# The attention loop of a hybrid encoder block, written out for its four head pairs

## The reference, cut to what matters

```python
MLA_HEADS, QK_NOPE_DIM, QK_ROPE_DIM, V_HEAD_DIM, CHUNK, Q_BLOCK = 8, 64, 32, 64, 64, 128
q = (rms_norm(q_c, q_norm_g) @ w_uq).reshape(B, S, H, 64 + 32)
kv = rms_norm(kv_c, kv_norm_g)
k_nope, v = kv @ w_uk, kv @ w_uv                  # per head 64 and 64 columns
...                                               # rotary part of q and k
s = (qn @ k_nope.T + qr @ k_rope.T) * sm_scale    # float32
s = where(key_chunk <= query_chunk, s, -1e30)     # block-causal, chunks of 64
out = softmax(s) @ v                              # per head and block of 128 queries
```

## Time and profile before

| | us |
|---|---|
| median of 3 runs | 2049.97 (2049.68 to 2051.54) |
| profiled execution | 2049.59 |
| its span, first to last instruction | 2047.8 |
| of which attention's steps | about 484 to 1105 |
| PE busy over the span | 1854.8 (91%) |
| DVE, ACT, POOL busy | 1220.7, 728.3, 499.6 |

### The profile page before, as it was taken

One profiled execution on the slowest core, in us unless ns is written; L12 is line 12 of the kernel. 1 busy time (PEld: TensorE's weight loads), 2 busy tenths in 40 slices (PEclk: granted clock), 3 DMA queues, 4 the chain that ended last, 5 costly groups with the idle time before them and its releaser, 6 DMA issues. The chain is left out here.

```text
span 2047.8 us, 27274 instructions
## 1 busy us (share of the span) xinstructions
PE 1854.8 (91%) x8738; PEld 1438.2 (70%) x8738; DVE 1220.7 (60%) x2093; ACT 728.3 (36%) x1209; POOL 499.6 (24%) x550
## 2 busy tenths in 40 slices
PE   2899999997999999999996999983999999999970
PEld 2677878764666666666664788872899999999960
DVE  4688889856675675675674655546344444444434
ACT  3545353325444444444443332320222222222214
POOL 0131413112211211211221111103234343434330
PEclk8999999997999999999998899985999999999995
DMA  7655656410000000000002434414799999999948
GB/s 275 203 176 153 202 139 181 144 56 1 9 8 6 8 8 5 8 8 5 8 8 100 174 139 145 159 73 154 240 271 275 271 270 278 267 280 270 276 98 328
DMA packets 216160, 290.79 MB, mean 142 GB/s; under 512 B 24373, under 2 KB 172048, under 8 KB 215834
## 3 DMA queue, kind: packets, MB, share of 16 engines
q1 hardware_dynamic: 193498, 220.60, 32.5%
q0 software_dynamic: 20224, 69.22, 13.5%
q10 hardware_dynamic: 2368, 0.17, 0.1%
HBM read 229.13 MB, written 60.82 MB: 142 GB/s over the span
## 5 line engine op out<-in xcount | busy, mean ns | idle before, releaser
L905 PE MATMUL tbank<-probs,VV 128*128 128x512 f32 (+3 forms) x640 | 292.5, 538 | 1.3 <-ACT probs L1123 1.2
L987 DVE TENSOR_REDUCE cmax<-tbank 128x1 f32<-128x512 f32 (+2 forms) x340 | 206.0, 606 | 99.1 <-PE tbank L830 91.9
L1123 ACT ACTIVATE probs<-tbank 128x512 f32<-128x512 f32 (+1 forms) x320 | 169.7, 533 | 235.3 <-PE tbank L876 231.6
L387 PE MATMUL pbank<-hhi,wslhi 128*128 128x512 f32 x512 | 205.9, 402 | 8.2 <-DVE wsllo L440 6.8
L874 PE MATMUL tbank<-Qhi,Khi 97*128 97x512 f32 (+2 forms) x321 | 212.4, 662 | 0.0
L1881 DVE TENSOR_SCALAR xTe<-ebank,modcol 128x256 f32<-128x256 f32 (+1 forms) x128 | 53.8, 473 | 258.8 <-PE ebank L1799 137.5
L1149 POOL TENSOR_SCALAR diag<-cst,nmax 128x128 fp32r<-128x128 f32 x138 | 84.4, 612 | 486.1 <-DVE nmax L990 485.8
L387 PE MATMUL pbank<-hhi,wsllo 128*128 128x512 f32 x512 | 200.7, 392 | 0.0
L387 PE MATMUL pbank<-hlo,wslhi 128*128 128x512 f32 x512 | 200.6, 392 | 0.0
L1821 PE MATMUL ebank<-xTe,wg 128*128 128x192 f32 x1024 | 171.8, 326 | 3.1 <-DVE ahi L1909 1.8
L1821 PEld LDWEIGHTS ebank<-xTe,wg 128*128 128x128 f32 x1024 | 167.9, 190 | 7.9 <-DVE ahi L1909 2.1
(11 more groups left out here) (273 smaller groups left out, 3491.4 us busy)
## 6 DMA issues: line engine op xcount, KB each, us to landing
wg<-in_w_exp_gate SPq DMA_DIRECT2D x32, 1024.0 KB, 6.3
wu<-in_w_exp_up SPq DMA_DIRECT2D x32, 1024.0 KB, 9.6
wd<-in_w_exp_down SPq DMA_DIRECT2D x32, 1024.0 KB, 7.4
wraw<-in_w_in SPq DMA_DIRECT2D x60, 512.0 KB, 4.1
wmod<-in_w_ada POOLq DMA_DIRECT2D x64, 256.0 KB, 3.4
xt<-in_x SPq DMA_DIRECT2D x4, 2048.0 KB, 11.0
wada<-in_w_ada SPq DMA_DIRECT2D x4, 2048.0 KB, 19.0
mixed<-mix_dram SPq DMA_DIRECT2D x16, 512.0 KB, 4.3
```

Source lines behind the costliest of these rows:

```text
L387: ins = pe.matmul(out, w[:, S % 3, k], h[:, n % 2, k], start=k == 0 and j == 0, stop=k == KD - 1 and j == 2)
L905: ins = pe.matmul(out, VV[:, kt, 2 * b:2 * b + 2].rearrange("p c d -> p (c d)"), step_of(probs, m), start=kt == 0, stop=last)
L987: W(ve.tensor_reduce(cmax[:, i % 2, n:n + 1], plain[:, chunk % 2, 0:w], AX.X, ALU.max), plain_read)
L1123: A(act.activation(step_of(probs, m), scores[:, m % 2, j * P:512], ACT.Exp), exp_done)
```

## The change

The loop over `hp` becomes a Python loop on PE, DVE, ACT and POOL, so four pairs are written out and the waits compare with constants. SP keeps its loop. A function `nothing_follows(hp, b)` is true for the last head of all. There the kernel leaves out all that prepares a further head. DVE's bookkeeping for loops goes: two waits for its own last instruction at places of the loop, and in `divide` the wait for the last instruction becomes a wait for the last product that read the tile `rs`.

```diff
+def nothing_follows(hp, b):
+    return (hp, b) == (HEADS // 2 - 1, 1)
...
-            with pe.Fori(0, HEADS // 2) as hp:
+            for hp in range(HEADS // 2):
                 for b in range(2):
                     head = hp * 2 + b
                     nxt = hp * 2 + (b + 1)
+                    end = nothing_follows(hp, b)
...
                         if m + LEAD < STEPS_HEAD:
                             score(m + LEAD, b, head)
-                        else:
+                        elif not end:
                             score(m + LEAD - STEPS_HEAD, 1 - b, nxt)
...
-                        if i % GQ == 0 and n == 0:
+                        if i % GQ == 0 and n == 0 and not (ahead and end):
                             pe.wait_ge(qlo_done, (nxt if ahead else head) * 4 + (i // GQ + 1))
-                        plain_scores(chunk, 1 - b if ahead else b, ...)
-                        if m in PART_AT:
+                        if not (ahead and end):
+                            plain_scores(chunk, 1 - b if ahead else b, ...)
+                        if m in PART_AT and not end:
...
-                        if (b, m) in V_AT:
+                        if (b, m) in V_AT and not end:
...
-                            spread_maxima(g, nxt if ahead else head)
+                            if not (ahead and end):
+                                spread_maxima(g, nxt if ahead else head)
...
 # vector: divide
                 if r == 0:
                     ve.wait_ge(out_free, head * GROUPS + (g + 2))
-                    W.wait()
+                    ve.wait_ge(divided, head * GROUPS + (g + 3))
...
 # vector: loop
-            with ve.Fori(0, HEADS // 2) as hp:
-                W.enter(hp, {...})
+            for hp in range(HEADS // 2):
...
-                        maximum(chunk_at(m)[0], ...)
-                        if m == 0:
+                        if not (ahead and end):
+                            maximum(chunk, ...)
+                        if m == 0 and not end:
                             W.wait()
                             weights(1 - b, hp * 2 + (b + 1))
...
-                    if b == 0:
-                        W.wait()
-                W.leave(HEADS // 2)
...
 # scalar and gpsimd: the same, act.Fori and po.Fori become range;
 # part, copy_values, copy_maxima, diagonal and rest only where `not end` allows them
```

More of the change, by code:

```diff
@@ L827, in plain_scores @@
                 w = key_cols(i, n)
-                if not (isinstance(seq, int) and seq < 2):
+                if seq >= 2:
                     pe.wait_ge(plain_read, seq - 1)
@@ L835, in spread_maxima @@
                 pe.wait_ge(diag_ready, head * NT + GQ * (g + 1))
-                if not (isinstance(head, int) and g == 0):
+                if head or g:
                     pe.wait_ge(neg_copied, head * GROUPS + g)
@@ L870, in score @@
                     pe.wait_ge(neg_copied, head * GROUPS + (g + 1))
-                if not (isinstance(head, int) and m < 2):
+                if head or m >= 2:
                     pe.wait_ge(exp_done, head * STEPS_HEAD + (m - 1))
@@ L916, in _ @@
                         i, n = CHUNK_OF[chunk]
-                        if i % GQ == 0 and n == 0:
+                        if i % GQ == 0 and n == 0 and not (ahead and end):
                             pe.wait_ge(qlo_done, (nxt if ahead else head) * 4 + (i // GQ + 1))
-                        plain_scores(chunk, 1 - b if ahead else b, hp * 2 * STEPS_HEAD + (b * STEPS_HEAD + AHEAD + m))
-                        if m in PART_AT:
+                        if not (ahead and end):
+                            plain_scores(chunk, 1 - b if ahead else b, hp * 2 * STEPS_HEAD + (b * STEPS_HEAD + AHEAD + m))
+                        if m in PART_AT and not end:
                             c = PART_AT[m]
@@ L1033, in _ @@
             W.wait()
-            with ve.Fori(0, HEADS // 2) as hp:
-                W.enter(hp, {dve_step: 2 * (3 + 4 + NT + GROUPS * 2), weights_ready: 2, made_dve: 16, qf_ready: 8,
-                             plain_read: 2 * STEPS_HEAD, max_ready: 2 * NT, divided: 2 * GROUPS})
+            for hp in range(HEADS // 2):
                 for b in range(2):
@@ L1039, in _ @@
                         g, kt = STEP_OF[m]
-                        maximum(chunk_at(m)[0], hp * 2 * STEPS_HEAD + (b * STEPS_HEAD + AHEAD + m))
-                        if m == 0:
+                        end = nothing_follows(hp, b)
+                        chunk, ahead = chunk_at(m)
+                        if not (ahead and end):
+                            maximum(chunk, hp * 2 * STEPS_HEAD + (b * STEPS_HEAD + AHEAD + m))
+                        if m == 0 and not end:
                             W.wait()
                             weights(1 - b, hp * 2 + (b + 1))
-                        if PART_AT.get(m - KEYS_AFTER, 1) % 2 == 0:
+                        if PART_AT.get(m - KEYS_AFTER, 1) % 2 == 0 and not end:
                             part(PART_AT[m - KEYS_AFTER], 1 - b, hp * 2 + (b + 1))
-                        if PART_AT.get(m, 0) % 2:
+                        if PART_AT.get(m, 0) % 2 and not end:
                             part(PART_AT[m], 1 - b, hp * 2 + (b + 1))
@@ L1116, in _ @@
             act.wait_ge(out_set, 1)
-            with act.Fori(0, HEADS // 2) as hp:
+            for hp in range(HEADS // 2):
                 for b in range(2):
@@ L1125, in _ @@
                             copy_out((g - 1) % GROUPS, hp * 2 + (b if g else b - 1))
-                        if PART_AT.get(m - KEYS_AFTER, 1) % 2 == 0:
+                        if PART_AT.get(m - KEYS_AFTER, 1) % 2 == 0 and not end:
                             part(PART_AT[m - KEYS_AFTER], 1 - b, hp * 2 + (b + 1))
-                        if PART_AT.get(m - QUERIES_SPLIT_AFTER, 0) % 2:
+                        if PART_AT.get(m - QUERIES_SPLIT_AFTER, 0) % 2 and not end:
                             part(PART_AT[m - QUERIES_SPLIT_AFTER], 1 - b, hp * 2 + (b + 1))
-                        if (b, m - 1) in V_AT:
+                        if (b, m - 1) in V_AT and not end:
                             copy_values(V_AT.index((b, m - 1)), hp + b)
@@ L1133, in _ @@
                             g, ahead = SPREAD_AT[m - 1]
-                            copy_maxima(g, 1 - b if ahead else b, hp * 2 + (b + ahead))
+                            if not (ahead and end):
+                                copy_maxima(g, 1 - b if ahead else b, hp * 2 + (b + ahead))
             copy_out(GROUPS - 1, HEADS - 1)
@@ L1160, in _ @@
                 diagonal(i, 0)
-            with po.Fori(0, HEADS // 2) as hp:
+            for hp in range(HEADS // 2):
                 for b in range(2):
@@ L1164, in _ @@
                         chunk, ahead = chunk_at(m)
-                        if chunk in TILE_END:
+                        end = nothing_follows(hp, b)
+                        if chunk in TILE_END and not (ahead and end):
                             diagonal(TILE_END.index(chunk), hp * 2 + (b + ahead))
-                        if PART_AT.get(m - QUERIES_REST_AFTER, 0) % 2:
+                        if PART_AT.get(m - QUERIES_REST_AFTER, 0) % 2 and not end:
                             rest(PART_AT[m - QUERIES_REST_AFTER] // 2, 1 - b, hp * 2 + (b + 1))
```

## The result

| | before | after |
|---|---|---|
| median of 4 runs | 2049.97 (2049.68 to 2051.54) | 2024.50 (2023.41 to 2025.00) |
| ratio | | 0.9873, 95% interval 0.9856 to 0.9891 |
| profiled execution, span | 2049.59, 2047.8 | 2023.41, 2021.6 |

The change gains 25.5 us (1.3%). I had said 2028.6, with a range from 2024.5.

The account below looks back on a forecast made before the run. PE was taken to bound attention. The last head's 18.0 us and the three turns' 3.2 make 21.2 off the profiled 2049.59, so 2028.4, stated as 2028.6 for the median; range 2024.5 to 2033.

Parts of the forecast that it names:

- the sum, 18.0 + 3.2: Whole kernel: 18.0 us from the last head plus 3.2 from three loop turns, 21.2 us gained.
- The prediction's own sign: Forecast counts as wrong if the first seven heads together change by more than 3.2 us.
- What bounds attention: In attention PE is full and sets the time; DVE and ACT have room.
- The last head: Work for a ninth head leaves PE: 18.5 us of slots less 0.5 of stalls, 18.0 net.
- The stalls: Last head: PE waits for an exponential 0.4 us at step 25 and 0.1 at step 39.
- Keys: Last head: four key parts leave PE at 1.01 us each, 4.0 us in all.
- the chain of maxima: Last head: 20 plain-score chunks, 3.70 us, plus next head's first score and two spreads, 1.2 us, leave PE.
- The turns: Between pairs of heads: PE's waits at three loop turns go, 1.08 us each, 3.2 us in all.
- The entry of the loop: Attention's start, ahead of the first turn: no gain counted, 0 us.
- The clock: Half-clock stretches before and after the loop may shift: 2 us allowed either way.
- more than I count: Rival: fewer register operations help PE or half-clock stretches shrink, giving 2025 us; chance 0.08.
- The price of longer code: PE in pairs 2 to 4: fetching some 15 more code packets costs 0 us.

Follow-up runs that it names:

- chain_only: The changed kernel, but its last head leaves out only the plain scores, maxima, diagonals, two spreads and first score for a ninth head; 2039.28 us, ratio to before 0.9942.
- dve_written: The kernel before with DVE's loop alone written out and nothing left out of the last head; 2047.17 us, ratio to before 0.9974.
- before_again: The kernel before, unchanged, run once more for a second profile; 2051.34 us, ratio to before 1.0003.
- pe_written: The kernel before with PE's loop alone written out and nothing left out of the last head; 2049.03 us, ratio to before 0.9992.

## Why the prediction was right in its main terms and failed at the loop's entry

The step that failed is the sum, 18.0 + 3.2. It counts the last head and the three turns and puts the entry of the loop, and all else ahead of the first turn, at nothing, without a reason. The runs showed 2.05 us there, from attention's first matmul to head 1's first exponential, of which 0.7 is the entry into the loop and 1.3 a shorter half-clock stretch. The prediction's own sign says the same: it is wrong "if the first seven heads grow or shrink together by more than the turns' 3.2", and they shrank by 4.5 counted from their first exponential and by 6.05 counted from attention's first matmul. What lies behind attention changed by 1.4 us, within the 2 us named. The parts in turn:

- *What bounds attention* was right: PE full, ACT and DVE not.
- *The last head*: 18.5 for 18.0. The stalls were right (0.39 at step 25, about 0.1 at step 39). Keys were priced by their own two matmuls, 1.01; removed, a step loses 1.2, which is 0.8 more for the four. Against that the chain of maxima, 4.9 in the sum, brought 4.3 in `chain_only`. That 18.0 came so near is partly these two errors cancelling.
- *The turns*: 4.00 for 3.2. Which waits go was right, and DVE's late code was their cause (`dve_written`). The price of a turn was read from a comparison in which I booked 0.71 us of work for the value part of a pair's first head. Written out the stretch shows 6.30 - 5.69 = 0.61, so a turn was 1.18 where I had 1.08. The first turn had cost 1.42 (its steps 2 and 3 took 0.2 longer than at the other turns, and the table load 0.05), which I didn't look at, and step 23's 0.07 comes on top three times.
- *The entry of the loop*: this is the missing term. I priced the three turns and said that one table load is left, and put the start at 0. It is 0.7 us, and with it went 1.3 us of half-clock time in the profiled execution.
- *The clock*: "I allow 2 us either way for them" was mis-sized and one allowance for two places. The start gave 1.3. The projection can take from 254.6 to 261.8 with the same instructions, and the changed kernel lands at 256.4 and 256.3. Against the profiled execution of before that is 0.5; against before_again 2.7. The median of before in larger samples is 2050.6 to 2052.3, so the few runs that I forecast from, 2049.97, were on its low side; with the larger samples the gain would look larger still.
- *The rival "more than I count"* with 2025 came closest, and had a chance of 0.08. It named half-clock stretches that shrink, which is 1.3 of the start, and a gain of PE's from fewer register operations, which is small: 0.07 us at step 23 of a pair's second head and about 0.2 us of waiting at the entry (`pe_written`).
- *The arithmetic*: 2028.4 and the 0.4 by which the median lies above the profiled execution make 2028.8, and I wrote 2028.6.
- *The price of longer code* was right at 0, and `pe_written` shows it alone.
- *A turn is not the price of its branch.* By the Trainium skill, "Advanced Engine Details and Errata", Control Flow Timing, three turns would have had 0.3 us; measured are 4.0. What the Trainium skill says in "Runtime: NRT & Kernel Launch", Instruction fetch mechanics, fits DVE's 3 us, which go where DVE has no branch.

Summed: the profiles differ by 26.2, the forecast had 21.2. Of the 5.0 missed the last head is 0.5, the turns 0.8, the start 2.05, the gap and the projection 1.1, and what lies ahead of attention and behind the projection 0.5.

What stays open: what decides where the half-clock stretches fall in an execution; whether the changed kernel meets the projection better than the one before or was lucky in eight runs; and the 0.55 us between last value and projection, a stretch of loads that took 18.2 to 19.0 in the profiles without added work.

## What to carry to other kernels

In this kernel a turn's cost lay with the engine whose next code wasn't there and with what it owed the bound engine soon after; look for "issue" in the waits, and price the entry like the turns. Writing out one engine's loop may bring nothing until the other's is written out too. Where a stage sits beside half-clock stretches, take its length from several profiles before a few us are put down to a change.

## What the runs showed of the hardware that I had not expected

- The same output projection took 254.6, 255.9, 256.4, 258.1, 259.1 and 261.8 us, with 6.8 to 20.5 us at 1.2 GHz within its third and fourth tile.
- An entry 0.3 to 0.5 us earlier went with a half-speed stretch of 23.9 instead of 27.3 us, 1.3 us of time, but only in the executions in which that stretch began 20.4 us or more behind attention's first matmul.
- At a turn of the loop the next instruction came 0.2 us behind the branch on ACT and POOL and 2.7 to 2.9 us behind it on DVE.
- Half-clock time in PE's waits cost at most 0.2 us; the same clock in the third tile of the projection cost 1.5 to 1.6 us for each further 3.4 us.
